# Prompt attention in blocks of split operands, and last pairs before each norm in the order of token blocks

## What is computed

```python
def rmsnorm(x, g):
    xf = x.astype(jnp.float32)
    y = xf * lax.rsqrt(jnp.mean(xf * xf, axis=-1, keepdims=True) + EPS)
    return (y * g.astype(jnp.float32)).astype(x.dtype)
...
c = jnp.cumsum(logf, axis=1)
...
s = jnp.einsum('bqhd,bkhd->bhqk', qi, k, preferred_element_type=jnp.float32) * scale
s = s + ci[:, :, :, None] - cT[:, :, None, :]
s = jnp.where(kpos[None, :] <= qpos[:, None], s, -jnp.inf)
pr = jax.nn.softmax(s, axis=-1)
return jnp.einsum('bhqk,bkhd->bqhd', pr.astype(v.dtype), v)
```

## Time and profile before

| | |
|---|---|
| device time, three runs | 3209.05, 3246.99 (median), 3280.55 us |
| the profiled execution | 3214.41 us, its span 3212.6 us |
| mean granted TensorE clock | 0.953 of 2.4 GHz |
| PE busy, weight loads busy | 90%, 83% of the span |
| DVE, ACT, POOL busy | 34%, 29%, 24% |
| mean DMA rate | 64 GB/s |

### The profile page before, as it was taken

How to read it: one execution, slowest core, us unless ns; L and a number is a source line. 1 busy time by engine, 2 the same in 40 slices (tenths; PEclk the granted TensorE clock), 3 DMA queues, 4 the chain that set the end, 5 groups by cost and what they waited for, 6 DMA issues and landing times.

```text
span 3212.6 us, 49548 instructions
## 1 busy us (share of the span) xinstructions
PE 2889.5 (90%) x18658; PEld 2679.4 (83%) x18658; DVE 1095.0 (34%) x1876; ACT 927.3 (29%) x1533; POOL 783.4 (24%) x378
## 2 busy tenths in 40 slices
PE   5787698999999999899999999788889999999997
PEld 4787487999999999799977777555789999999997
DVE  6899635111111112511124555434351111111114
ACT  4555533211112112311124454322232211111113
POOL 2899423222122212311100000000022221222221
PEclk8888799999999999999978999999899999999999
DMA  3110011111111111224212011499311111111111
GB/s 95 32 34 26 27 40 33 42 43 46 39 53 38 48 46 34 65 75 127 64 33 75 20 27 46 139 309 310 113 33 46 36 51 42 41 52 32 54 36 71
DMA packets 243438, 206.66 MB, mean 64 GB/s; under 512 B 18189, under 2 KB 218893, under 8 KB 243077
## 3 DMA queue, kind: packets, MB, share of 16 engines
q1 hardware_dynamic: 229895, 184.56, 18.9%
q10 hardware_dynamic: 13453, 20.90, 2.0%
HBM read 183.16 MB, written 23.13 MB: 64 GB/s over the span
## 4 chain that ended last, share of the span: by engine, by line
PE 52%; issue 31%; POOL 8%; DVE 6%; ACT 2%; DMA 1%; DVEq 0%; ACTq 0%; SPq 0%; POOLq 0%
PE PS L659 17%; PE PS L661 17%; PE PS L660 17%; POOL yp L615 7%; DVE tm L1517 2%; POOL wlo L592 1%; DVE rs L1496 1%; DMA xin<-in_x_prompt 1%; DVE hlo L1559 1%; PE PS L786 0%; DVE xlo L1502 0%; ACT prods L1230 0%; ACT tm L1272 0%; ACT xhi L1128 0%; DVE u L1611 0%
## 5 line engine op out<-in xcount | busy, mean ns | idle before, releaser
L659 PE MATMUL PS<-xhi,whi 128*128 128x352 f32 x3456 | 1144.5, 331 | 132.1 <-DVE u L1611 46.0
L661 PE MATMUL PS<-xlo,whi 128*128 128x352 f32 x3456 | 1121.6, 325 | 0.0
L660 PE MATMUL PS<-xhi,wlo 128*128 128x352 f32 x3456 | 1121.3, 324 | 0.0
L592 POOL TENSOR_TENSOR wlo<-wraw,whi 128x1024 fp32r<-128x1024 f32 x208 | 498.4, 2397 | 1839.2 <-ACT whi L1117 1839.2
L659 PEld LDWEIGHTS PS<-xhi,whi 128*128 128x128 f32 x3456 | 657.7, 190 | 176.7 <-DVE u L1611 55.7
L660 PEld LDWEIGHTS PS<-xhi,wlo 128*128 128x128 f32 x3456 | 660.6, 191 | 0.0
L661 PEld LDWEIGHTS PS<-xlo,whi 128*128 128x128 f32 x3456 | 658.8, 191 | 0.0
L1117 ACT ACTIVATE whi<-wraw 128x1024 fp32r<-128x1024 f32 x208 | 218.9, 1052 | 594.2 <-PE PS L661 565.8
L1554 DVE TENSOR_TENSOR ht<-PS,ht 128x352 f32<-128x352 f32 x132 | 69.1, 525 | 906.3 <-PE PS L661 902.3
L659 PE MATMUL PS<-hhi,whi 128*128 128x352 f32 x1056 | 341.2, 323 | 8.8 <-issue 8.8
L660 PE MATMUL PS<-hhi,wlo 128*128 128x352 f32 x1056 | 338.7, 321 | 0.0
(11 more groups left out here) (184 smaller groups left out, 2424.3 us busy)
## 6 DMA issues: line engine op xcount, KB each, us to landing
wraw<-in_ffn_w_gu SPq DMA_DIRECT2D x88, 512.0 KB, 3.8
kr<-in_cache_k SPq DMA_DIRECT2D x64, 512.0 KB, 8.2
vr<-in_cache_v SPq DMA_DIRECT2D x64, 512.0 KB, 9.4
wraw<-in_ffn_w_down SPq DMA_DIRECT2D x32, 384.0 KB, 3.4
wraw<-in_attn_w_in SPq DMA_DIRECT2D x24, 512.0 KB, 4.0
wraw<-in_ffn_w_down SPq DMA_DIRECT2D x32, 320.0 KB, 3.2
wraw<-in_conv_w_in SPq DMA_DIRECT2D x16, 512.0 KB, 4.1
wraw<-in_conv_w_out SPq DMA_DIRECT2D x8, 512.0 KB, 4.1
```

What stands on the lines that cost most here:

```text
L592: nc.gpsimd.tensor_tensor(wlo[:, s, :], wraw[:, s, :], whi[:, s, :].bitcast(F32), ALU.subtract).then_inc(w_lo, 1)
L659: nc.tensor.matmul(out, wh, hi[:, k, blk(b)], start=(k == 0), stop=False)
L660: nc.tensor.matmul(out, wl, hi[:, k, blk(b)], start=False, stop=False)
L661: m = nc.tensor.matmul(out, wh, lo[:, k, blk(b)], start=False, stop=(k == kc - 1))
```

## The change

**Attention.** Queries, keys and the cumulative gate are split where they are staged: ACT rounds `stg` into `sth`, POOL subtracts into `stl`, and each goes to a scratch of its own. DVE splits the gate into `chi` and `clo`. The score of a tile is now two fp32r products over 128 and 66 rows (query high against key low and key high, then query low against key high with two rows of ones against the gate), plus a 128-column product of the identity and the mask on the diagonal, which replaces DVE's addition. SP loads the operands in 15 transfers before the first tile and 24 for each later pair, in quarters and halves that are free. The tiles alternate between the two heads, from the last 128 queries to the first. POOL scales the probabilities in place by the reciprocal of their sum. The transposes follow three tiles behind the scores. ACT copies the transposed probabilities of key tiles 0 to 3, DVE those from 4 on; tiles with fewer than 4 go to ACT for the first head and to DVE for the second. The value product of 256 queries and both heads (a block) runs with V as the stationary operand, 64 columns, head 0 into PSUM partitions 0 to 63 and head 1 into 64 to 127, in three portions over later tiles; the result needs no transpose. All eight pairs are written out. K pages now start to load after the attention, and the first unit of the output projection in the midst of the requests.

**Norms.** The last pair before each norm runs in the order of token blocks, and the sums, root, reciprocal and chunks of block 0 stand in the queues ahead of the work of block 2. The sum of block 2 comes after the first half-block of the next pair. That opening pair has extra weight buffers `whx`, `wlx` for its slot 1, and in blocks 1 and 2 PE goes chunk by chunk through both slots. The low parts of chunks 0, 3 and 6 are DVE's, the other five POOL's.

```diff
+            def load_queries(i, c0, signal):
+
+                cols = slice(c0, c0 + QW)
+                sp.dma_start(qa[0:DH, :, cols].bitcast(F32), pair(q_hi, i, cols)).then_inc(signal, 16)
+                sp.dma_start(qa[DH:P, :, cols].bitcast(F32), pair(q_hi, i, cols)).then_inc(signal, 16)
+                sp.dma_start(qb[0:DH, :, cols].bitcast(F32), pair(q_lo, i, cols)).then_inc(signal, 16)
...
+            def load_top(i, c0):
+
+                cols, keys = slice(c0, c0 + QW), slice(c0 - HALF, c0 - HALF + QW)
+                sp.dma_start(kau[0:DH, :, keys].bitcast(F32), pair(k_lo_scr, i, cols)).then_inc(a_up, 16)
+                sp.dma_start(kau[DH:P, :, keys].bitcast(F32), pair(k_hi_scr, i, cols)).then_inc(a_up, 16)
+                sp.dma_start(kbu[0:DH, :, keys].bitcast(F32), pair(k_hi_scr, i, cols)).then_inc(a_up, 16)
+                sp.dma_start(kbu[DH:DH + 2, :, keys].bitcast(F32), c_scr[:, 2 * i:2 * i + 2, cols]).then_inc(a_up, 16)
...
+            for i in range(1, C):
+
+                sp.wait_ge(a_sc, NTAU * (i - 1) + 4)
+                load_queries(i, SEQ - QW, a_up)
+                load_top(i, SEQ - QW)
+                sp.wait_ge(a_sc, NTAU * (i - 1) + 8)
+                load_top(i, HALF)
+                load_queries(i, HALF, a_mid)
+
+                sp.wait_ge(a_sc, NTAU * i)
+                load_lower(i)
+                if i + 1 < C:
+                    load_keys(i + 1)
...
+            sp.wait_ge(a_pv, NBLOCKS)
             for n in range(4):
                 load_k(n)
...
+            def opening_lows(q, n, before_slot0):
+
+                pool.wait_ge(w_hi, q * 2 + 1)
+                nc.gpsimd.tensor_tensor(wlx[:, :], wraw[:, 1, :], whx[:, :].bitcast(F32), ALU.subtract).then_inc(w_lo, 1)
+                norm_lows(n, 0, range(before_slot0))
+                pool.wait_ge(w_hi, q * 2 + 2)
+                nc.gpsimd.tensor_tensor(wlo[:, 0, :], wraw[:, 0, :], whi[:, 0, :].bitcast(F32),
+                                        ALU.subtract).then_inc(w_lo, 1)
+                norm_lows(n, 0, range(before_slot0, C))
+                for b in range(1, NB):
+                    norm_lows(n, b)
             low_parts(0)
...
+            def staged_lows(q):
+
+                for s in range(2):
+                    pool.wait_ge(w_hi, q * 2 + (s + 3))
+                    nc.gpsimd.tensor_tensor(wlo[:, s, :], wraw[:, s, :], whi[:, s, :].bitcast(F32),
+                                            ALU.subtract).then_inc(w_lo, 1)
+
+                    pool.wait_ge(qk_hi, q * 2 + (s + 1 - 2 * Q_ATTN_IN))
+                    nc.gpsimd.tensor_tensor(stl[:, s, :], stg[:, s, 0:SEQ], sth[:, s, :].bitcast(F32),
+                                            ALU.subtract).then_inc(qk_lo, 1)
...
+            for g in range(TILES):
+                i, h, qt = tile(g)
+                pool.wait_ge(a_rec, g + 1)
+                probs = pr[:, g % 4, 0:(qt + 1) * P]
+                nc.gpsimd.tensor_scalar(probs, probs, rden[:, g % NTAU:g % NTAU + 1], None, ALU.mult).then_inc(a_nrm, 1)
...
+            def closing_pair(q, kc, hi, lo, r):
+
+                for b in range(NB):
+                    for s in range(2):
+                        if b == 0:
+                            pe.wait_ge(w_lo, q * 2 + (s + 1))
+                        unit_block(q, s, b, kc, hi, lo)
+                        if b == 1 and s == 0:
+                            norm_sum(r, 0)
+                norm_sum(r, 1)
...
+            def opening_pair(q, hi, lo, before, r):
+
+                pe.wait_ge(w_lo, q * 2 + 2)
+                unit_block(q, 0, 0, C, hi, lo, before)
+                norm_sum(r, 2)
+                unit_block(q, 1, 0, C, hi, lo, extra=True)
+                for b in range(1, NB):
+                    for s in range(2):
+                        pe.wait_ge(ev[s], seen(s, q - 1, b))
+                    for k in range(C):
+                        before(b, k)
+                        for s in range(2):
+                            out = PS[:, NB * s + b, 0:BW]
+                            wh, wl = weights(s, k, s == 1)
+                            nc.tensor.matmul(out, wh, hi[:, k, blk(b)], start=(k == 0), stop=False)
+                            nc.tensor.matmul(out, wl, hi[:, k, blk(b)], start=False, stop=False)
+                            m = nc.tensor.matmul(out, wh, lo[:, k, blk(b)], start=False, stop=(k == C - 1))
+                            if k == C - 1:
+                                m.then_inc(mm[s], 1)
+
+            def pairs(q0, n, kc, hi, lo, before=None, abreast=False, opens=None, closes=None):
...
+                q1, q2 = qa[:, h, qt * P:(qt + 1) * P], qb[:, h, qt * P:(qt + 1) * P]
+                for k0 in range(0, nk, HALF):
+                    n = min(nk - k0, HALF)
+                    out = PS[:, 2 * (g % 2) + k0 // HALF, 0:n]
+                    k1, k2 = (kau[:, h, 0:n], kbu[:, h, 0:n]) if k0 else (kal[:, i % 2, h, 0:n], kbl[:, i % 2, h, 0:n])
+                    last = k0 + n == nk
+                    nc.tensor.matmul(out, q1, k1, start=True, stop=False)
+                    nc.tensor.matmul(out, q2, k2, start=False, stop=not last)
+                m = nc.tensor.matmul(PS[:, 2 * (g % 2) + qt // 4, (qt % 4) * P:(qt % 4 + 1) * P], identr[:, :],
+                                     cmaskr[:, :], start=False, stop=True)
+                m.then_inc(a_sc, 1)
+
...
+            def prompt_values(n, part):
+                i, bn = block_of(n)
+                if part == 0:
+                    pe.wait_ge(a_pta, NA[4 * n + 4])
+                    pe.wait_ge(a_ptd, ND[4 * n + 4])
+                    past(pe, o_ev, n - 1)
+                for kt in portions(n)[part]:
+                    c0 = P if kt == 2 * bn + 1 else 0
+                    for h in range(2):
+                        m = nc.tensor.matmul(PS[DH * h:DH * h + DH, 6 + n % 2, c0:QW],
+                                             Vt[:, kt, (2 * i + h) * DH:(2 * i + h + 1) * DH],
+                                             block_probs(n)[:, h, kt, c0:QW], start=(kt == 0),
+                                             stop=(kt == 2 * bn + 1), skip_group_check=True)
+                if part == 2:
+                    m.then_inc(a_pv, 1)
...
+            for g in range(TILES + 6):
+                if g < TILES:
+                    prompt_scores(g)
+                if g >= 7:
+                    n, part = divmod(g - 7, 4)
+                    if part < 3:
+                        prompt_values(n, part)
+                if 3 <= g < TILES + 3:
+                    probs_tr(g - 3)
...
+                square(0, 0)
+                square(1, 0)
+                square(0, 1)
+                norm_root(r, 0)
...
+                act.wait_ge(w_ld[1], q * 16 + 32)
+                nc.scalar.activation(whx[:, :], wraw[:, 1, :], ACT.Copy).then_inc(w_hi, 1)
+                if short:
+                    next_hi(q, 0)
+                    square(1, 1)
+                    norm_hi(n, 0, range(1))
+                    norm_root(r, 1)
+                    norm_hi(n, 0, range(1, C))
+                else:
+                    square(1, 1)
+                    norm_hi(n, 0, range(3))
+                    next_hi(q, 0)
+                    norm_hi(n, 0, range(3, C))
+                    norm_root(r, 1)
+                square(0, 2)
+                square(1, 2)
+                norm_hi(n, 1, range(4))
+                norm_root(r, 2)
+                norm_hi(n, 1, range(4, C))
+                norm_hi(n, 2)
...
+            def store_staged(q, s, hi, lo, q0):
+
+                u = (q - Q_ATTN_IN) * 2 + s
+                past(act, stg_st[s], (q - Q_ATTN_IN) * 32)
                 act.wait_ge(ev[s], seen(s, q, NB - 1))
+                nc.scalar.activation(sth[:, s, :], stg[:, s, 0:SEQ], ACT.Copy).then_inc(qk_hi, 1)
+                rows = ds(q * (2 * P) + (s * P - q0 * 2 * P), P)
+                act.wait_ge(qk_hi, u + 1)
                 act.nop(nofuse=True)
-                act.dma_start(scr[ds(q * (2 * P) + (s * P - q0 * 2 * P), P), :], stg[:, s, 0:SEQ]
-                              ).then_inc(stg_st[s], 16)
-
-            with act.Fori(Q_ATTN_IN, QK) as q:
+                act.dma_start(hi[rows, :], sth[:, s, :].bitcast(F32)).then_inc(stg_st[s], 16)
+                act.wait_ge(qk_lo, u + 1)
+                act.nop(nofuse=True)
+                act.dma_start(lo[rows, :], stl[:, s, :].bitcast(F32)).then_inc(stg_st[s], 16)
...
+            def prompt_exp(g):
+                i, h, qt = tile(g)
+                nk = (qt + 1) * P
+                act.wait_ge(a_max, g + 1)
+                if g >= 4:
+                    if uses(g - 4)[1]:
+                        act.wait_ge(a_trd, ND[g - 4] + 1)
+                    else:
+                        act.wait_ge(a_tra, NA[g - 4] + 1)
+                t = g % NTAU
+                nc.scalar.activation(pr[:, g % 4, 0:nk], banks(2 * (g % 2), nk), ACT.Exp,
```

(17 more changed lines are left out.)

644 lines of the change are left out of this document (368 added, 276 removed).

## The result

The changed kernel takes 3134.68 us (median of four runs, 3130.41 to 3137.17) against 3228.02 for the kernel before in the same session. The ratio, taken over the fast runs of both, is 0.9748 (95% interval 0.9709 to 0.9787). It is faster. But it sits 45 us above the number, and 10 us above the 3060 to 3125 of my own account; only the wider range of 3030 to 3170 holds it. Between the profiled executions (3214.41 and 3137.17) it gained 77 us, where my sum had 126. Of the 108 us predicted for the attention, 96 are there. Of the 27 us predicted for the norms, 3.5 can be found.

What follows compares the result with a forecast made beforehand. The prediction took PE to bound feed-forward and attention, DVE to pace the norms. 3214.4 - 108 (attention) - 27 (norms) + 7 (K pages) + 2 (gate split) = 3088, say 3090; range 3060 to 3125, wider 3030 to 3170.

Steps and rivals of the forecast that it cites:

- The attention, -108: Attention stage: falls from 389 to 281 us, at 31 us a pair of heads at full clock.
- PE's sum, 26.3 us a pair: Attention: PE's work per pair of heads, 10.3 scores and masks, 8.4 transposes, 7.6 overlapping value products.
- in series: Attention rival: the two heads' value products do not overlap, a pair takes 38.8 us, total 3152; chance 0.12.
- POOL's scaling, 12 us: Attention: POOL scales the probabilities in 12 us a pair, bounds 8.1 to 21.6, covered by PE's 26.3.
- Stalls of 4.9: Attention: PE's stalls stay at today's 4.9 us a pair, giving 31 us a pair.
- The half clock of 61 us: Attention start: the clock stays at half for 61 us as before, while 1.16 pairs are done.
- clock at once: Attention rival: the clock comes back at once, 25 us less, total 3065; chance 0.20.
- The start, 3 us: Attention start: DVE's first maximum waits for the eight cb_scr stores, 3 us later, including a 2 us landing.
- the clock stay down: Attention rival: PE stays at 1.2 GHz, 52.6 us a pair, stage +40 us, total 3236, slower; chance 0.08.
- The norms, -27: The four norms: starting block 0's norm early saves 9.2 us twice, 4.8 before the attention, 3.4 at the last.
- Projections: Query and key projections: the gate split adds 2 us; doubled ACT and POOL work stays covered.
- K pages, +7: Requests stage: the first four K pages load after the attention, 2 MB more at 285 GB/s, 7 us.

Runs made afterwards that it cites:

- kernel with thin scaling: The changed kernel, but POOL scales only the first 128 columns of each tile of probabilities; a pair of heads took 32.1 us.
- broadcast form: The changed kernel, but POOL scales by a tensor_tensor multiplication with the reciprocal broadcast along the columns, not a tensor_scalar; 3117.58 us.
- the control: The kernel before with two added memsets and a later attention start, score matmuls still reading 65 rows; attention 405.7 us.
- the kernel with the norms undone: The changed kernel with the four norms after residual pairs as they were before; 3133.92 us.
- combined kernel: The changed kernel with a later wait for the cb_scr stores, two-input POOL scaling, old order at norm 2 and two ACT order moves; 3097.67 us.

## Why the prediction was right, and where it wasn't

**The attention, -108 against -96.4 (290.2 us, from the first score to the last value product, against 281).** The mechanism held: shorter products, and two heads' values at once. That the number is near is in part luck, since two misses cancel.
- *PE's sum, 26.3 us a pair.* In the kernel with thin scaling, I gave the time from one record's start to the next to the first of the two. The value products take 9.5 us (7.6 had), the scores 10.1 (8.4), the masks 3.3 (1.9) and the transposes 9.2 (8.4), together the pair's 32.1. Each includes the switch to the next group and its stalls. The stalls are some 3.4 of it by my estimate, 1.2 of them one wait for an exponential, so PE's own part is about 28.7. The column halves overlap, as the step had it. The rival "in series" is out: made so, a pair takes 41.05 us.
- *POOL's scaling, 12 us, bounds 8.1 and 21.6.* **This is the term that was mis-sized**: it measured 27.4. The upper bound came from a two-input instruction, in the belief that one tensor could not cost more than two. It does: from 128 to 1024 columns the per-partition scalar form grows by (2.842 - 0.602)/896 = 2.50 ns a column, the broadcast form by (1.892 - 0.613)/768 = 1.67. The 26.3 us of PE behind which I hid it were too little, and it came into the open at the long tiles, 2.1 us a pair.
- *Stalls of 4.9.* Some 3.4 were left without POOL's part. With PE's larger sum the pair is then 32.1 against my 31.
- *The half clock of 61 us.* It was 24. The rival "clock at once" was nearer. The step that failed took one trace's 61 us for a property of the chip, when the control shows 27 and 82 for nearly the same work. Eight pairs at 34.2 instead of 31 cost 26 us; 61 us at half clock for 1.16 pairs would have cost 25 more than they did at full speed, and about 20 of these came back.
- *The start, 3 us.* Right wait, wrong size: the landing took 11.3 us, not 2. The trace of the kernel before shows most of it, and I hadn't looked there: the same eight stores (0.52 MB) move with no other transfer beside them, at 37 GB/s, and their last packet ends at 1662.4, 7.7 us after the last is issued at 1654.7. Nothing waited for them then. In the changed kernel, loads of the operands run beside them (2.9 MB from 1655 to 1685) and the last packet ends at 1677.4. So 7.7 us is the stores' own; that the loads are the rest is likely and wasn't tried apart.

The Trainium skill (GPSIMD Engine Reference, 3.1 Elementwise) has a short one-input body at 1.03 cycles an element; from it came my estimate of 8 us a pair. The trace disagrees: 2.50 ns a column is some three times that at the page's 1.2 GHz. By the rule on transposes that I named (the Trainium skill, TensorE: Matmul & The Clock Gate, Part 4: PE-mode transpose) I had the clock stay down as a rival. It didn't: from 1688 on it is 1.00 with a third of PE's records transposes. As the other two thirds are products, this says little on the rule itself.

**The norms, -27 against -3.5 (-3.4, +4.2, -3.9, and -0.4 at the end against the kernel with the norms undone).** This step failed. I followed DVE's queue in the right order and left out four things around it. The figures are of one trace: over the traces with all the new norms, norm 2 takes 90.1 to 94.5 us. T is the moment at which block 0 of the last pair before a norm (the closing pair) is done, 480.5 at the first norm.
- *The closing pair needs both slots' weights at once.* The order of blocks asks for slot 1's weights after one block of slot 0 (2.4 us at 5 chunks, 3.85 at 8) instead of three. POOL's low part is late:

```profile
1287.47 0.43 PE L797 MATMUL PS<-hhi,whi 128*128 128x352 f32 x1 [2.45 <-POOL wlo L694]
```

 The wait is 2.45 us there and before the last norm, 1.11 at the first.
- *POOL's weight subtractions hold DVE up* (2.68 us for 0.5 above). DVE is through block 0's chunks 21.5 us after T at the first norm, not 19.1, and everything behind them is later too, to the opening pair's end at T+48.7, not T+45. The Trainium skill (SBUF — State Buffer, Who interferes with whom) calls the port pair that DVE and POOL share an exclusive lock, and says that a DVE instruction with two inputs in SBUF contends with a POOL instruction that reads SBUF; the 2.68 and the 1.06 us agree.
- *The wait behind each opening pair was right* (3.91, 3.18, 3.91; 3.6 had), but not the half clock that follows it:

```profile
534.30:537.60 3.30, 3.30 (x13) 3.30 (x12) 1.72 (x2) 0.00 (x0) 0.89 (x1) 0.50 0.78 222
1339.90:1346.60 6.70, 5.96 (x20) 5.96 (x21) 0.00 (x0) 2.01 (x2) 5.04 (x3) 0.50 0.74 254
```

 The granted clock falls to 0.50 after it, now in a stretch that PE alone paces. By my estimate that costs 1.6 and 2.8 us. The old norm had one such stretch of 10.2 us, in which DVE set the pace anyway. The new one has two or three of 3.4 or 6.8.
- *The last norm* gave back its 3.4 us by the closing pair's wait of 2.45 and the 3.4 us at half clock behind it.

**Projections, +11.0 against +2.** I called the doubled ACT and POOL work hidden, and in the steady pairs it is: 11.45 us a unit, before and after. It shows at the seams, the places between two kinds of work where PE needs something that ACT makes once. There ACT's wait for POOL's staged low part stands ahead of the gate weights:

```profile
1415.88 2.35 POOL L748 TENSOR_TENSOR stl<-stg,sth 128x1024 fp32r<-128x1024 f32 x1
...
1418.89 0.31 ACT L1527 ACTIVATE wfs<-wfr 128x128 fp32r<-128x128 f32 x1 [4.43 <-POOL stl L748]
```

PE's gaps there and before the transposes of the new tokens' queries and keys grew from 3.71 to 7.16 and from 1.49 to 4.91 us. The gate split took 1.4 (2 had). Most of what remains is half clock behind the gaps (10.2 us at 0.50 after the first, 3.4 in the kernel before). The combined kernel took both gaps back, the second in part, by order alone.

**K pages, +7 against +11.3 (9.4 and 1.9 of the first wait).** At 284 GB/s the 2 MB of pages give 7. I had read in the change that the first weights of the output projection move into the same stage, and costed it nowhere: four loads of 512 KB stand there now for two before, another 3.7 by the same rate. The stage moves 71.1 MB for 68.0, which is these 3 MB. The 1.9 us stand in the attention's row of the ledger. This part wasn't tried apart.

**Against the rivals:** "clock at once" was near on the clock and wrong on the time, since POOL took its gain. Hand-offs at 40 us a pair, series at 38.8 and the clock that stays down didn't happen.

## What to carry to other kernels

A stretch at half clock in one trace is a sample; look at the spread of the runs before pricing it. A transfer for which nobody waits today can be waited for tomorrow: its own queue in today's trace tells how long it takes. Bound an engine's unknown instruction by the same form, not by one that reads more: the form with a scalar per partition cost more than the one with two tensors, and the cover it hid behind must be compared with that bound. When work is doubled on an engine with room, look at its seams, the places where its in-order queue feeds another engine once, not at its steady loop. An order of work that shortens one long wait by making several short ones pays for each in clock and in buffers that come free late.
